# Linear attention: q and k of the next head are scaled beside this one, and each head's result is normed and gated from its bank

## The reference, cut to what matters

```python
b = cumsum(log_a over the chunk); b_last = b[..., -1:, :]
q_t   = q * exp(b)
k_t   = k * exp(-b)
k_end = k * exp(b_last - b)
attn     = where(mask, q_t @ k_t.T, 0)
o_intra  = attn @ v
chunk_kv = k_end.T @ v
state    = decay * state + chunk_kv      # from chunk to chunk
o_inter  = q_t @ state_before_the_chunk
```

```python
o = rms_norm(o, out_gain).reshape(bsz, seq, B_V_WIDTH)   # over each head's 256 values
o = o * silu(r)
return o @ w_out
```

## Time and profile before

| | us |
|---|---|
| median of 3 runs | 1904.08 (1903.54 to 1905.59) |
| the profiled execution, its own time | 1899.7 |
| its span from the first to the last instruction | 1898.4 |
| PE busy in it | 1688.8 (89%) |
| DVE busy | 1140.5 (60%) |
| ACT busy | 860.0 (45%) |
| POOL busy | 243.4 (13%) |

### The profile page before, as it was taken

How to read it: one execution, slowest core, us unless ns; L and a number is a source line. 1 busy time by engine, 2 the same in 40 slices (tenths; PEclk the granted TensorE clock), 3 DMA queues, 4 the chain that set the end, 5 groups by cost and what they waited for, 6 DMA issues and landing times. The chain is left out here.

```text
span 1898.4 us, 25087 instructions
## 1 busy us (share of the span) xinstructions
PE 1688.8 (89%) x10106; PEld 1468.6 (77%) x10106; DVE 1140.5 (60%) x1462; ACT 860.0 (45%) x1055; POOL 243.4 (13%) x205
## 2 busy tenths in 40 slices
PE   4998999989999987689999899958979879989988
PEld 3777888879987865589988688647879768779976
DVE  3877676755544456555546864338887555567754
ACT  5344655644434552344444333445544444345543
POOL 1553340000000000000001600004444100000000
PEclk9999999989999998799999999978989989989999
DMA  5453435645655353256544323000000065445533
GB/s 194 161 177 112 133 122 188 198 130 180 191 172 191 116 164 121 67 169 186 181 164 140 119 54 105 22 17 1 1 1 1 2 201 176 162 150 173 180 134 122
DMA packets 161906, 240.97 MB, mean 127 GB/s; under 512 B 12640, under 2 KB 80992, under 8 KB 161664
## 3 DMA queue, kind: packets, MB, share of 16 engines
q1 hardware_dynamic: 154400, 232.81, 37.7%
q10 hardware_dynamic: 7104, 4.64, 0.8%
q0 software_dynamic: 288, 1.92, 0.3%
HBM read 238.29 MB, written 1.05 MB: 126 GB/s over the span
## 5 line engine op out<-in xcount | busy, mean ns | idle before, releaser
L197 DVE TENSOR_TENSOR wlo<-raw,whi 128x2048 fp32r<-128x2048 f32 x224 | 524.3, 2352 | 320.2 <-ACT whi L191 306.8
L191 ACT ACTIVATE whi<-raw 128x2048 fp32r<-128x2048 f32 x224 | 420.3, 1886 | 313.0 <-PE ps L328 269.3
L326 PE MATMUL ps<-xs,whi 128*128 128x256 f32 (+1 forms) x1312 | 387.7, 296 | 17.9 <-DVE xs L457 7.7
L327 PE MATMUL ps<-xs,whi 128*128 128x256 f32 (+1 forms) x1312 | 386.2, 294 | 0.0
L328 PE MATMUL ps<-xs,wlo 128*128 128x256 f32 (+1 forms) x1312 | 386.0, 294 | 0.0
L326 PE MATMUL ps<-whi,xs 128*128 128x512 f32 x672 | 274.5, 408 | 35.9 <-DVE wlo L197 19.6
L326 PEld LDWEIGHTS ps<-xs,whi 128*128 128x128 f32 x1312 | 250.4, 191 | 26.9 <-issue 20.4
L327 PE MATMUL ps<-wlo,xs 128*128 128x512 f32 x672 | 269.2, 401 | 0.0
L328 PE MATMUL ps<-whi,xs 128*128 128x512 f32 x672 | 269.1, 400 | 0.0
L327 PEld LDWEIGHTS ps<-xs,whi 128*128 128x128 f32 x1312 | 250.5, 191 | 5.7
L328 PEld LDWEIGHTS ps<-xs,wlo 128*128 128x128 f32 x1312 | 250.3, 191 | 5.8
(11 more groups left out here) (365 smaller groups left out, 2384.4 us busy)
## 6 DMA issues: line engine op xcount, KB each, us to landing
raw<-in_ffn_w_gate_up SPq DMA_DIRECT2D x88, 512.0 KB, 4.7
raw<-in_a_w_in SPq DMA_DIRECT2D x72, 512.0 KB, 4.6
raw<-in_w_in SPq DMA_DIRECT2D x60, 512.0 KB, 4.5
raw<-in_w_mod SPq DMA_DIRECT2D x48, 512.0 KB, 4.7
raw<-in_w_up SPq DMA_DIRECT2D x44, 512.0 KB, 4.7
raw<-in_ffn_w_down SPq DMA_DIRECT2D x40, 512.0 KB, 4.6
raw<-in_b_w_in SPq DMA_DIRECT2D x24, 512.0 KB, 4.5
raw<-in_w_down SPq DMA_DIRECT2D x20, 512.0 KB, 4.1
```

What stands on the lines that cost most here:

```text
L191: self.hi_ok.inc(act.activation(self.whi[:, h % NHI, 0:nk, :], self.raw[:, h % NRAW, 0:nk, :], ACT.Copy))
L197: self.lo_ok.inc(dve.tensor_tensor(self.wlo[:, h % NRAW, 0:nk, :], self.raw[:, h % NRAW, 0:nk, :], self.whi[:, h % NHI, 0:nk, :].bitcast(F ...
L326: pe.matmul(o, ahi, bhi, start=start, stop=False)
L327: pe.matmul(o, ahi, blo, start=False, stop=False)
```

## The change

There are now two sets of `qd`, `kd` and `ke`, used by the heads in turn. The scalings become a function `scale_qk(h)`; that of head 0 stands ahead of the memsets, that of head h+1 behind the states of head h. `M.out` and `W.lo` of a head change places. The copy of the product into `o` goes away. In its place ACT squares and sums the two tiles of the product from their banks and takes the root, and DVE takes the reciprocal of two columns and writes bank by root by gated gain into `r`. The gain is multiplied into `r` beforehand on POOL, in two halves, as soon as ACT has written each. `gate_act` and `gate_dve` are gone, and the transposes read `r`.

```diff
-        qd, kd, ke = c(2, SEQ), c(2, SEQ), c(2, SEQ)
+        qd_, kd_, ke_ = ([c(2, SEQ) for _ in range(2)] for _ in range(3))
         rows = c(CW)
-        o = c(TT, VW)
+        sq, st = c(TT, GLA_DV), c(GLA_HEADS, TT)
...
+                qd, kd, ke = qd_[h % 2], kd_[h % 2], ke_[h % 2]
                 pe.wait_ge(lb_qk.sem, h + 1)
...
                 for half in nxt[h]:
                     W.hi(half)
+                for t in range(TT):
+                    act.wait_ge(lb_o.sem, 2 * h + t + 1)
+                    as_.inc(act.activation(sq[:, t], ps[:, 6 + t, 0:GLA_DV], ACT.Square, scale=GLA_DV ** -0.5, accum_out=st[:, h, t:t + 1]))
+                act.wait_ge(as_.sem, as_.n)
+                lb_rt.inc(act.activation(st[:, h], st[:, h], ACT.Sqrt, bias=eps_col))
+
+        def heads_pool():
+
+            pool.wait_ge(rows_in.sem, rows_at)
+            for j in range(2):
+                pool.wait_ge(lb_evac.sem, 5 + j)
+                half = slice(j * CW, (j + 1) * CW)
+                lb_gr.inc(pool.tensor_tensor(r[:, :, half], r[:, :, half], bc(gain[:, half], 1, TT), ALU.mult))
+
+        def scale_qk(h):
+            hs = slice(h * SEQ, (h + 1) * SEQ)
+            qd, kd, ke = qd_[h % 2], kd_[h % 2], ke_[h % 2]
+            for d in range(2):
+                dve.tensor_tensor(qd[:, d, :], qT[:, h, :], e1[:, d, hs], ALU.mult)
+                dve.tensor_tensor(kd[:, d, :], kT_[:, h, :], e2[:, d, hs], ALU.mult)
+                i_ = dve.tensor_tensor(ke[:, d, :], kT_[:, h, :], e3[:, d, hs], ALU.mult)
+            lb_qk.inc(i_)
 
         def heads_dve():
             mid.meet(dve)
+            scale_qk(0)
             dve.memset(AT, 0.0)
...
                 if h:
                     dve.wait_ge(lb_o.sem, 2 * h)
-                for d in range(2):
-                    dve.tensor_tensor(qd[:, d, :], qT[:, h, :], e1[:, d, hs], ALU.mult)
-                    dve.tensor_tensor(kd[:, d, :], kT_[:, h, :], e2[:, d, hs], ALU.mult)
-                    i_ = dve.tensor_tensor(ke[:, d, :], kT_[:, h, :], e3[:, d, hs], ALU.mult)
-                lb_qk.inc(i_)
                 dve.wait_ge(lb_att.sem, h + 1)
...
+                if h + 1 < GLA_HEADS:
+                    scale_qk(h + 1)
+                M.out(8 + h, 5)
                 for half in nxt[h]:
                     W.lo(half)
-                M.out(8 + h, 5)
+                dve.wait_ge(lb_rt.sem, h + 1)
+                vs.inc(dve.reciprocal(st[:, h], st[:, h]))
+                dve.wait_ge(vs.sem, vs.n)
+                dve.wait_ge(lb_gr.sem, 1 + h // 2)
                 for t in range(TT):
-                    dve.wait_ge(lb_o.sem, 2 * h + t + 1)
-                    lb_out.inc(dve.tensor_copy(o[:, t, hv], ps[:, 6 + t, 0:GLA_DV]))
+                    lb_out.inc(dve.scalar_tensor_tensor(r[:, t, hv], ps[:, 6 + t, 0:GLA_DV], st[:, h, t:t + 1], r[:, t, hv],
+                                                        ALU.mult, ALU.mult))
...
-        split_and_add(lambda t, k: o[:, t, k * P:(k + 1) * P], 0, out_chunks, nxt_chunk, norm)
+        heads_pool()
+        split_and_add(lambda t, k: r[:, t, k * P:(k + 1) * P], 0, out_chunks, nxt_chunk, norm)
```

More of the change, by code:

```diff
@@ L1270, in build @@
     lb_g, lb_ke, lb_att, lb_kv, lb_o = (Signal(nc, "pe", "b_" + n) for n in ("gates", "ke_transposed", "scores", "kv", "product"))
-    lb_ln, lb_ex, lb_evac, lb_kt, lb_sq = (Signal(nc, "act", "b_" + n) for n in ("gate_ln", "decays", "evacuated", "kt", "squares"))
-    lb_qk, lb_at, lb_s, lb_out, lb_sum = (Signal(nc, "dve", "b_" + n) for n in ("qk_scaled", "masked", "states", "out", "sum"))
+    lb_ln, lb_ex, lb_evac, lb_kt = (Signal(nc, "act", "b_" + n) for n in ("gate_ln", "decays", "evacuated", "kt"))
+    lb_qk, lb_at, lb_s, lb_out = (Signal(nc, "dve", "b_" + n) for n in ("qk_scaled", "masked", "states", "out"))
+    lb_gr = Signal(nc, "pool", "b_gain")
     lb_rt = Signal(nc, "act", "b_root")
@@ L1501, in heads_dve @@
             for h in range(GLA_HEADS):
-                hs, hv = slice(h * SEQ, (h + 1) * SEQ), slice(h * GLA_DV, (h + 1) * GLA_DV)
+                hv = slice(h * GLA_DV, (h + 1) * GLA_DV)
                 if h:
                     dve.wait_ge(lb_o.sem, 2 * h)
-                for d in range(2):
-                    dve.tensor_tensor(qd[:, d, :], qT[:, h, :], e1[:, d, hs], ALU.mult)
-                    dve.tensor_tensor(kd[:, d, :], kT_[:, h, :], e2[:, d, hs], ALU.mult)
-                    i_ = dve.tensor_tensor(ke[:, d, :], kT_[:, h, :], e3[:, d, hs], ALU.mult)
-                lb_qk.inc(i_)
                 dve.wait_ge(lb_att.sem, h + 1)
@@ L1540, in layer_b @@
         heads_dve()
-        fin = Stage()
-        sq, st = e1.rearrange("p a b -> p (a b)"), dec.rearrange("p a b -> p (a b)")
-        nh = TT * GLA_HEADS
-        def gate_act():
-            fin.meet(act)
-            lb_sq.inc(act.activation(sq, o.rearrange("p a b -> p (a b)"), ACT.Square, scale=GLA_DV ** -0.5))
-            act.wait_ge(lb_sum.sem, 1)
-            lb_rt.inc(act.activation(st[:, 0:nh], st[:, 0:nh], ACT.Sqrt, bias=eps_col))
-        def gate_dve():
-            fin.meet(dve)
-            dve.wait_ge(lb_sq.sem, 1)
-            lb_sum.inc(dve.tensor_reduce(st[:, 0:nh], sq.rearrange("p (n d) -> p n d", d=GLA_DV), AX.X, ALU.add))
-            dve.wait_ge(lb_rt.sem, 1)
-            dve.wait_ge(rows_in.sem, rows_at)
-            vs.inc(dve.reciprocal(st[:, 0:nh], st[:, 0:nh]))
-            dve.wait_ge(vs.sem, vs.n)
-            o3 = o.rearrange("p a (n d) -> p (a n) d", d=GLA_DV)
-            vs.inc(dve.tensor_tensor(o3, o3, bc(st[:, 0:nh], 2, GLA_DV), ALU.mult))
-            dve.wait_ge(vs.sem, vs.n)
-            vs.inc(dve.tensor_tensor(o, o, bc(gain, 1, TT), ALU.mult))
-            dve.wait_ge(vs.sem, vs.n)
-            vs.inc(dve.tensor_tensor(o, o, r, ALU.mult))
-        gate_act()
-        gate_dve()
-        split_and_add(lambda t, k: o[:, t, k * P:(k + 1) * P], 0, out_chunks, nxt_chunk, norm)
+        heads_pool()
+        split_and_add(lambda t, k: r[:, t, k * P:(k + 1) * P], 0, out_chunks, nxt_chunk, norm)
     mg_bc, mg_out = Signal(nc, "pe", "mod_gates_spread"), Signal(nc, "act", "mod_gates_out")
```

## The result

The changed kernel took 1877.07 us (median of 4 runs, 1872.08 to 1885.13), the kernel before beside it 1903.81 us (1896.47 to 1905.59). The ratio is 0.9871, with a 95% interval of 0.9827 to 0.9915. The forecast was 1883.6 us. Timed a second time the ratio was the same, 0.9871, with an interval of 0.9856 to 0.9886 (1878.86 against 1904.52 us, 25.7 us between the medians, 24.6 by the ratio). The time fell by the 20.5 us of the sum and 4 to 6 us more.

The account below looks back on a forecast made before the run. PE's work in the heads plus the waits in which it stands still was taken as the bound. Gains of 8.9 + 10.0 + 0.6 + 1.0 = 20.5 us from the 1904.1 us median gave 1883.6 us, range 1876 to 1889.

Parts of the forecast that it names:

- the 20.5 us of the sum: Whole kernel: total forecast gain, 8.9 for pauses, 10.0 for the tail, 0.6 for head 0's start, 1.0 for the clock.
- The pauses at the boundaries: PE's three waits for scalings between heads, 2.54 + 3.78 + 2.54 us, would go: 8.9 us gained.
- The cover of the low parts: Low parts behind the scalings finish before the next head's M.acc needs them, by 0.3 and 0.0 us at full clock: cost nothing.
- The rival in which PE comes to wait for low parts: PE waits in M.acc of heads 1 to 3: 17.5 us gained, or 16.0 at 1.5 us each; chance 15%.
- Squares, root and passes beside the next head: On ACT and DVE behind each head's product, all hidden by 2 to 4 us beside the next head's work.
- The rival that ends slower: Root some 12 us late, so passes, masks, states and product stand in one line: 1908 us or more; chance 3%.
- P: The time at which a head's product is finished; root expected at P + 1.3, in head 0 at P + 2.6.
- The tail: PE's wait for the gate behind the last head falls from 12.78 to 2.8 us: 10.0 us gained.
- The start of head 0: Memsets move behind the scalings, POOL's multiplication runs beside them: 0.6 us gained, 1.6 if DVE isn't slowed, -0.2 at x1.86.
- The clock: In heads and transposes behind the gate, fewer PE pauses win back time lost to the low clock: 1 us, between 0 and 11.2.
- the forecast's own bounds: Whole kernel's median time with 18 to 23 us gained: 1881 to 1886 us; chance 62%.
- The rest moves up as a whole: What follows the change is released by PE's progress, so it was expected simply to start earlier; no size given.

Follow-up runs that it names:

- the scalings alone: Only two sets of qd, kd, ke and scalings behind the states, with old copies, norm and gate, against the kernel before: 1893.50 us, ratio 0.9945.
- half of `M.acc` in the pause: Changed kernel with M.acc's second half behind the chunk states' matmuls, M.cols behind the product: 0.9834; POOL's second multiplication also moved 0.9806; last gate first too 0.9813.
- The norm from the bank alone: Only norm and gate from the banks, gain on POOL, one set of qd, kd, ke, against the kernel before: 1892.15 us, ratio 0.9938.
- the filler: Changed kernel plus four unread matmuls per head in the pause ahead of the product: 1876.96 us, 0.9860 of before; with POOL's second multiplication moved, 0.9843.

## Why the prediction was right, step by step

**The pauses at the boundaries** (8.9 us). Right, to the last: none is left in either profile of the changed kernel. With the scalings alone the time fell by 10.5 us, of which the start is 1.65 us (3.99 less 2.34).

**The cover of the low parts** (nothing to pay). Right. The rival in which PE comes to wait for low parts did not occur. In the heads at full clock of the second profile, where the cover was reckoned at 0.3 and 0.0 us, it was 0.4 and 0.1 us: in head 2 the low parts end at 737.80 and 740.05, and PE's first matmuls with them begin at 738.22 and 740.19. The waits of PE from 722 to 751 us hold nothing but the pause ahead of the product (line, releaser, us in total, times, longest):

```profile
PE ps L1470 <- issue: 4.4, 2, 2.2
```

**Squares, root and passes beside the next head.** Right. The table load stands in head 0 at 1.28 us, the root directly behind it, and the masks begin at 726.49 us, 4.68 us ahead of the states' first copy (731.17). The rival that ends slower needed a root that is 12 us late; it was at P + 2.2 in head 0, where 2.6 had been reckoned, and DVE waited 0.74 us for it. In both profiles of the changed kernel the squares waited for the product and not for high parts. In the three kernels with half of `M.acc` in the pause the high parts start later and the first square of each head stands directly behind them, but the second still begins within 0.2 us of the product's end.

**The tail** (10.0 us). Right, a little better: 2.25 us are left and not 2.8, so 10.5 us. The hops had been put at 0.15 to 0.26 us; the first four of the five are 0.03 to 0.05 us, and the last, from DVE to PE, is 0.28. The norm from the bank alone gave 11.8 us in time (9.1 to 14.3).

**The start of head 0** (0.6 us gained, between -0.2 and 1.6). Wrong, in sign too: 0.5 us were lost, outside the bounds. The step that failed is the price of DVE beside POOL. I took a factor of 1.46 over the six scalings, 0.5 us for each. What happened is that one scaling stood for 2.2 us, and the other five took 0.41 us: the price is a wait for the end of POOL's instruction and not a factor. The bound should have been the whole length of POOL's instruction (2.34 us) on top of 2.1 us. The rows that gave the factor say so too when they are read one by one, as the last section shows. The experiment that moves POOL away gives 2.34 us for the start and shows the cause. Of the Trainium skill's rule ("GPSIMD Engine Reference", Specifications), that DVE instructions with two SBUF inputs contend with GpSimd, the direction is confirmed, and a row agrees with its condition: in the kernel with the norm alone a memset, which has no input, took 0.27 us beside POOL, its usual time.

**The clock** (1 us, between 0 and 11.2). This is the term that was mis-sized, and what moved the result off the forecast's own bounds. In the heads and the transposes behind them it measured -1.5 us in the first profile (68.2 us for the heads where before had 66.2, and 0.5 us back in the transposes), which is outside the bounds, and +5.5 in the second (61.2 us). The lower bound of 0 rested on a misread row: I took the product of 4.92 us in head 0 for one at the low level, but its window (715.99 to 720.91 us) has a granted clock of 0.65, so it ran there only in part. A product wholly at the low level takes 6.1 us, as three heads of the first profile show, and so a head could also get longer. That the clock falls in or behind the pause ahead of the product was right, and the filler shows it. By the ratio 24.6 - 18.8 = 5.8 us came from here, or from what I can't separate from it: the parts outside the stretch differ by up to 9.6 us from profile to profile. The 1 us stood for a term that measures -1.5 or 5.5 us in single executions; that the forecast lies only 4.7 and 6.5 us from the two medians owes something to luck.

**The rest moves up as a whole.** Right for the work: the changed kernel's rest is 1104.5 and 1104.3 us, before 1103.6. But over the twelve profiles it wandered between 1102.2 and 1108.4 us, without one instruction changed, and the part ahead of the heads between 696.2 and 701.4.

What stays open: where the 6 us of the median beyond the fixed parts come from, why heads of the same program take 14.1 us in one execution and 16.9 in another, and whether the 2.2 us at the start show in the time of the kernel without filler. All three would need many profiles of each kernel.

## What to carry to other kernels

Look at each pause of PE for what ends it, and ask not only whether a second buffer would permit an earlier start, but where in the other engine's queue the work then stands: ahead of the low parts it was worth 8.9 us, behind them half of that came back as a wait. When two engines may get in each other's way, look at single rows and at when each began before taking a factor from a total. Take work that needs a result away from the end of a stage if the result lies in a bank tile by tile: 12.8 us of norm and gate became 2.3. And when PE has a pause left that recurs in a loop, put half of a neighbouring product into it before anything else; it pays the pause and keeps the clock, 2.7 us a head here where the clock fell, on top of the pause itself.

## What the runs showed of the hardware that was not expected

A DVE instruction with two SBUF inputs that starts together with a POOL instruction may stand until that one is over: 2.61 us for 0.42 us of work beside a POOL multiplication of 2.34 us, in both profiles of the changed kernel, and three more kernels show the same start of 4.5 us. Started 1.7 us later beside the same instruction it took 0.96 us, again to 0.28 us after POOL's end (timeline of the kernel with the norm alone):

```profile
699.95 2.34 POOL L1507 TENSOR_TENSOR wide<-wide 128x1024 f32<-128x1024 f32 x1 [9.80 <-ACT wide L1369]
...
701.61 0.96 DVE L1513 TENSOR_TENSOR wide<-wide 128x256 f32<-128x256 f32 x1
```

Yet the earlier trace rows has a low part that starts 0.09 us ahead of POOL and keeps its 2.29 us; of the two POOL instructions that begin there the first takes 3.35 us and the second 1.28. The other rows, taken one by one in the trace of before (shortest, median and longest in ns, first and last start in us), fit the same reading:

```profile
L197 DVE TENSOR_TENSOR wlo<-raw,whi x2: 3380/3382/3383, 52.6 to 55.9; 128x2048 fp32r<-128x2048 f32 x2
L924 POOL TENSOR_TENSOR wide<-wide x2: 1736/1738/1739, 50.4 to 52.1; 128x512 f32<-128x512 f32 x2
L929 POOL TENSOR_TENSOR wide<-wide x2: 3227/3284/3342, 53.9 to 57.1; 128x512 f32<-128x512 f32 x2
```

The first low part begins at 52.57 us inside a POOL instruction that ends at 53.80, and is done at 55.95, 2.15 us behind that end. Alone it takes 2.29 us, so 0.14 more, and by the same 0.14 us a scaling that takes 0.42 us alone ends 0.28 us behind POOL's. The POOL instruction that began at 53.88 then ends at 57.1, and the second low part 2.15 us behind that, at 59.26. In all these rows the instruction that came first went through, and the one that came together with or behind it stood until it was over, whichever engine it was on. All of them are DVE instructions with two SBUF inputs beside multiplications and additions on POOL; no run varies either kind alone.

TensorE's clock fell to 0.50 in the product behind a pause of 2.9 us (2.2 us of it idle, the rest four tiny matmuls), stayed there for all 6.1 us of a product in which PE was busy throughout, and was at 1.00 in the 2.4 us of transposes and scores behind it (740.20 to 742.60 us of the first profile). The same pause in the second profile of the same program left it at 1.00 in two heads. With 1.97 us of filler in the pause it didn't fall in any of the heads behind the first.
